# Modulation weights issued by GpSimd, the first token half routed inside the second half's output product, and second-map weights in another row order

## The reference, cut to what matters

```python
sh1, sc1, g1, sh2, sc2, g2 = split(silu(c) @ w_mod + b_mod, 6)   # w_mod 1024 x 6144
u = rmsnorm(x) * (1 + sc1) + sh1                                 # the context likewise
x_rnn, g_rnn, x_pool, m_rnn, m_pool = split(u @ w_in)
h = recurrent_states(x_rnn)          # 4 heads x 2 directions, gates by lru_wa, lru_wx
y_rnn = (h_f + h_b) * gelu(g_rnn);   y_pool = pool_mixer(x_pool)
merged = sigmoid(m_rnn) * (y_rnn @ w_rnn_proj) + sigmoid(m_pool) * (y_pool @ w_pool_proj)
x = x + g1 * rmsnorm(merged @ w_out)
v = rmsnorm(x) * (1 + sc2) + sh2
top_v, top_i = top_k(v @ w_r + b_r, 4)                           # of 32 experts
for e in range(32):
    z = v @ w1[e] + b1[e]            # 1024 x 2048
    act = clamped_swiglu(z)
    out += comb[:, e] * (act @ w2[e] + b2[e])                    # 1024 x 1024
x = x + g2 * rmsnorm(out)
```

## Time and profile before

| what | us |
|---|---|
| median of 3 runs (lowest, highest) | 1409.52 (1408.44, 1411.38) |
| the profiled execution | 1408.91 |
| its span | 1407.2 |
| TensorE busy | 1294.5 (92%) |
| VectorE busy | 348.0 (25%) |
| ScalarE busy | 215.9 (15%) |
| GpSimd busy | 19.3 (1%) |

### The profile page before, as it was taken

The page is one execution under the profiler, slowest core; times in us unless marked ns, Lnnn a source line. Parts: engine busy times, 40 slices in busy tenths (PEclk is TensorE's granted clock), DMA queues, the critical chain, the costliest instruction groups (busy, mean ns, idle before and its releaser), DMA issues.

```text
span 1407.2 us, 13120 instructions
## 1 busy us (share of the span) xinstructions
PE 1294.5 (92%) x5600; PEld 553.8 (39%) x5600; DVE 348.0 (25%) x605; ACT 215.9 (15%) x357; POOL 19.3 (1%) x58
## 2 busy tenths in 40 slices
PE   4999995699979999999999999999999999999995
PEld 2445684578643333333333333322333322333331
DVE  2457675332251112111211121111121111121112
ACT  3167530030011001000100010000010000010001
POOL 1000000000000000000000000000000000000000
PEclk9999997899968999999999999999999999999999
DMA  9322438999447999999999999999999999999994
GB/s 351 96 90 90 135 120 301 344 336 356 171 183 277 415 419 416 416 418 418 418 416 416 416 418 417 417 418 417 416 417 418 418 418 416 416 417 418 417 418 194
DMA packets 116905, 488.56 MB, mean 347 GB/s; under 512 B 9104, under 2 KB 43088, under 8 KB 79984
## 3 DMA queue, kind: packets, MB, share of 16 engines
q1 hardware_dynamic: 114768, 485.18, 86.2%
q0 software_dynamic: 544, 2.10, 0.4%
q10 hardware_dynamic: 1536, 0.46, 0.1%
HBM read 486.65 MB, written 1.05 MB: 347 GB/s over the span
## 4 chain that ended last, share of the span: by engine, by line
PE 43%; DMA 40%; DVE 6%; ACT 6%; SPq 4%; issue 1%; DVEq 0%; ACTq 0%
DMA arena<-in_exp_w 35%; PE bank L658 16%; PE bank L670 7%; PE bank L583 6%; SPq L361 3%; DMA arena<-in_w_in 3%; DMA arena<-in_w_mod 2%; PE bank L640 2%; PE bank L572 2%; PE bank L513 2%; PE bank L704 2%; PE bank L681 2%; ACT arena L822 1%; ACT arena L824 1%; ACT L816 1%
## 5 line engine op out<-in xcount | busy, mean ns | idle before, releaser
L658 PE MATMUL bank<-arena,temps 128*64 128x512 f32 x2112 | 472.8, 595 | 33.0 <-DMA arena<-in_exp_w 33.0
L658 PEld LDWEIGHTS bank<-arena,temps 128*64 128x64 f32 x2112 | 145.8, 137 | 354.4 <-issue 255.1
L670 PE MATMUL bank<-arena,temps 128*64 128x512 f32 x1056 | 233.9, 595 | 0.6 <-DVE temps L1239 0.6
L1232 DVE TENSOR_SCALAR temps<-bank 128x512 f32<-128x512 f32 x33 | 22.8, 692 | 750.1 <-PE bank L658 750.1
L583 PE MATMUL bank<-arena 128*128 128x256 f32 x512 | 119.2, 396 | 28.9 <-DMA arena<-in_w_in 28.9
L670 PEld LDWEIGHTS bank<-arena,temps 128*64 128x64 f32 x1056 | 72.6, 137 | 138.5 <-issue 132.5
L583 PEld LDWEIGHTS bank<-arena 128*128 128x128 f32 x512 | 101.9, 200 | 47.2 <-issue 32.3
L894 ACT ACTIVATE temps<-temps 128x512 f32<-128x512 f32 x33 | 20.8, 629 | 560.7 <-DVE temps L1232 560.7
L640 PE MATMUL bank<-vtokb,hot 128*64 128x512 f32 x264 | 67.4, 633 | 0.7 <-DVE hot L1174 0.7
L681 PE MATMUL bank<-temps,hot 64*128 64x512 f32 x264 | 65.6, 615 | 0.8 <-ACT temps L900 0.8
L704 PE MATMUL bank<-b1r,bsel 128*64 128x512 f32 x264 | 62.3, 592 | 0.6 <-issue 0.6
(11 more groups left out here) (229 smaller groups left out, 789.9 us busy)
## 6 DMA issues: line engine op xcount, KB each, us to landing
arena<-in_exp_w SPq DMA_DIRECT2D x396, 1024.0 KB, 22.0
arena<-in_w_mod SPq DMA_DIRECT2D x24, 1024.0 KB, 9.0
arena<-in_w_in SPq DMA_DIRECT2D x20, 1024.0 KB, 7.8
arena<-in_w_pool_proj SPq DMA_DIRECT2D x4, 1024.0 KB, 8.0
arena<-in_w_rnn_proj SPq DMA_DIRECT2D x4, 1024.0 KB, 6.6
arena<-in_w_out SPq DMA_DIRECT2D x4, 1024.0 KB, 10.2
arena<-in_lru_wa SPq DMA_DIRECT2D x8, 256.0 KB, 2.8
arena<-in_lru_wx SPq DMA_DIRECT2D x8, 256.0 KB, 3.1
```

Source lines behind the costliest of these rows:

```text
L658: last = mm(psum[4 + q][h * SLOTS:(h + 1) * SLOTS, :], xg[:, k // 4, k % 4, :], wslot[s][:, q, h * HALF:(h + 1) * HALF], start=False, stop ...
L670: last = mm(psum[6][h * SLOTS:(h + 1) * SLOTS, :], actT[:, k // 4, k % 4, :], wslot[s][:, kk, h * HALF:(h + 1) * HALF], start=(k == 0), st ...
L1232: v.tensor_scalar(glu, psum[4][:, :], LIMIT, None, ALU.min).then_inc(glu_ready, 1)
```

## The change

1. `gm` leaves `front_plan()` and the ring. GpSimd issues the 16 transfers after its constants, into four slots (`GM_SLOTS`: `ROWS_AT`, `M2`, `XC`, `XC + 1`), each once the product on that slot's former contents is done; from the eighth on (`GM_EARLY` = 7) also after the recurrence (`lru_done` = 8), since `XC` holds its input. VectorE does products 0 to 2 after the first three `conv`, 3 to 6 after steps 4 to 7, the rest after the pooling windows. ScalarE waits for `gm_done` = 7 before it writes `mp` into `M2`.
2. The product of the last quarter (t = 1, h = 1) is cut: k 0 and 1, then `vt` of half 0, k 2 to 5, `lg` of half 0, k 6 and 7, `rk` of half 0. ScalarE and VectorE take their parts in that order. `rk` becomes two jobs.
3. Ranks are kept from 1 and not from 0: `slotno` counts from 1 and the subtraction of 1 goes. `one_hot(0, 0)` moves ahead of the weights `comb`, and `neg_max` behind the mask.
4. Second-map weights: partition p holds rows 2p and 2p + 1 of each 256, and no longer rows p and 128 + p; the four turns of `actf` read every second column to match.

```diff
-RING_CHUNKS = 4 + 2 * HEADS + 4 + 12 + 16 + 1 + 8
-GM_AFTER = [0, 0, 1, 1, 2, 2, 2, 2, 2, 2, 1, 1]
+RING_CHUNKS = 4 + 2 * HEADS + 4 + 12 + 1 + 8
+GM_SLOTS = [ROWS_AT, M2, XC, XC + 1]
+GM_AT = [0, 1, 0, 1, 0, 1, 0, 2, 3, 0, 2, 3, 0, 2, 3, 0]
+GM_EARLY = 7
...
-        plan += [("vt", 2 * t, "A"), ("vt", 2 * t + 1, "V"), ("lg", t, "V")]
-    plan += [("rk", 0, "V"), ("ct", 0, "V")]
+        plan += [("vt", 2 * t, "A"), ("vt", 2 * t + 1, "V"), ("lg", t, "V"), ("rk", t, "V")]
+    plan += [("ct", 0, "V")]
...
-            return I["exp_w2"][0, ds(e, 1), r:r + 256, :].rearrange("a (k p) n -> p (a k) n", p=P)
+            return I["exp_w2"][0, ds(e, 1), r:r + 256, :].rearrange("a (p k) n -> p (a k) n", p=P)
...
-            link(g.iota(iotaI[:, :], pattern=[[64, 4], [0, 2], [1, 64]], base=0, channel_multiplier=0))
+            link(g.iota(iotaI[:, :], pattern=[[64, 4], [0, 2], [1, 64]], base=1, channel_multiplier=0))
...
+            pool.wait_ge(mod_used, KT)
+            for n in range(16):
+                k, h, q = n // 2, n % 2, GM_AT[n]
+                if n == GM_EARLY:
+                    pool.wait_ge(lru_done, 2 * HEADS)
+                if q in GM_AT[:n]:
+                    pool.wait_ge(gm_done, max(m for m in range(n) if GM_AT[m] == q) + 1)
+                pool.dma_start(slot(GM_SLOTS[q]), w_mod[k * P:(k + 1) * P, (h + 1) * CW:(h + 2) * CW]).then_inc(gm_landed[q], 16)
...
+                        wo(0, 0)
+                        wo(0, 1)
+                        wo(1, 0)
+                        wo(1, 1, 0, 2)
...
                     if n == 0:
+                        wo(1, 1, 2, 6)
                         pe.wait_ge(late_landed, 16 * 6)
...
+                elif kind == "rk" and n == 0:
+                    wo(1, 1, 6, KT)
+                    pe.wait_ge(mask_ready, 1)
+                    end_job(mm(b[:, 0:E], upper[:, :], mask[:, 0, :], start=True, stop=True))
                 elif kind == "rk":
...
+                    mm(b[:, 0:E], ones[:, :], mask[:, 0, :], start=True, stop=False)
+                    pe.wait_ge(mask_ready, 2)
+                    mm(b[:, 0:E], upper[:, :], mask[:, 1, :], start=False, stop=True)
+                    mm(b[:, E:2 * E], ones[:, :], mask[:, 0, :], start=True, stop=False)
+                    end_job(mm(b[:, E:2 * E], ones[:, :], mask[:, 1, :], start=False, stop=True))
...
-                    turned = nc.tensor.transpose(psum[7][:, j * P:(j + 1) * P], actf[:, j * P:(j + 1) * P], ident[:, :])
+                    turned = nc.tensor.transpose(psum[7][:, j * P:(j + 1) * P], actf[:, j // 2 * 256 + j % 2:j // 2 * 256 + 256:2], ident[:, :])
...
+                if kind == "mp":
+                    act.wait_ge(gm_done, GM_EARLY)
...
+            square_mix(0, 0)
+            square_mix(0, 1)
+            roots(0)
+            square_mix(1, 0)
+            take_turned(0)
+            square_mix(1, 1)
+            roots(1)
+            take_turned(1)
...
+            def mod_product(n):
+
+                k, h, q = n // 2, n % 2, GM_AT[n]
+                dve.wait_ge(gm_landed[q], 16 * GM_AT[:n + 1].count(q))
...
             for j in range(4):
                 conv(j)
+                if j < 3:
+                    mod_product(j)
...
                     conv(s + 4)
+                else:
+                    mod_product(s - 1)
...
+            for n in range(GM_EARLY, 16):
+                mod_product(n)
...
+            mix_half(0, 0)
+            tokens_of(0)
+            mix_half(1, 0)
+            route(0)
+            tokens_of(1)
+            take_rank(0)
+            route(1)
+            b = take_rank(1)
+            one_hot(0, 0)
+            v.tensor_copy(cnt, b[0:MORE, E:2 * E]).then_inc(read_dve, 1)
             dve.wait_ge(exps_ready, TT)
...
-            link(v.scalar_tensor_tensor(rank[:, :], b[:, 0:64], 1.0, mask.rearrange("p t e -> p (t e)"), ALU.add, ALU.mult))
-            link(v.tensor_scalar(rank[:, :], rank[:, :], -1.0, None, ALU.add))
```

More of the change, by code:

```diff
@@ L73, in front_plan @@
         plan += [("lru", s, None), ("xr", s + 4, "A") if s < 4 else ("xp", s - 4, "A")]
[L74 to L79, removed]
+    for kind in ("gg", "mr", "mp"):
+        plan += [(kind, c, "A") for c in range(4)]
     plan += [("pw", g, "A") for g in range(4)]
@@ L224, in build @@
         mod_landed = [sem(f"mod_landed{n}") for n in range(KT)]
+        gm_landed = [sem(f"gm_landed{q}") for q in range(4)]
         mod_used, mod_turned, gm_done, uT_act, uT_dve = (
@@ L503, in arrive, with wo @@
                 return chunk_of(kind, n)
[L505 to L513, removed]
-                                      wo_w[k // 2][:, k % 2, h * HALF:(h + 1) * HALF], start=(k == 0), stop=(k == KT - 1))
-                        last.then_inc(wo_done, 1)
+            def wo(t, h, k0=0, k1=KT):
+                for k in range(k0, k1):
+                    last = mm(psum[2 * t + h][:, :], mgT[:, k, t * P:(t + 1) * P],
+                              wo_w[k // 2][:, k % 2, h * HALF:(h + 1) * HALF], start=(k == 0), stop=(k == KT - 1))
+                if k1 == KT:
+                    last.then_inc(wo_done, 1)
             def mod_columns(k0, k1):
@@ L875, in _, with take_turned @@
                 a.activation(stat[:, 24 + t:25 + t], stat[:, 22 + t:23 + t], ACT.Sqrt).then_inc(root3, 1)
-            for t in range(TT):
+            def take_turned(t):
                 b = job_of("vt", 2 * t)
@@ L1117, in _, with one_hot, weighted, mix_half @@
                 v.tensor_tensor(m1[:, r], m1[:, r], m2[:, r], ALU.add).then_inc(merged_ready, 1)
-            for t in range(TT):
-                for h in range(2):
-                    dve.wait_ge(ssq2_ready, 2 * t + h + 1)
-                    r = slice(h * HALF, (h + 1) * HALF)
-                    ins = v.tensor_tensor(mG[:, t, r], psum[2 * t + h][:, :], row["g1"][:, r], ALU.mult)
+            def one_hot(e, r):
+                for t in range(TT):
+                    ins = v.tensor_scalar(sel[:, t, :], slotno[:, ds(r * 128, SLOTS)], rank[:, ds(e + t * E, 1)], None,
+                                          ALU.is_equal)
+                ins.then_inc(sel_ready, 1)
+            def weighted(e, r):
+                for t in range(TT):
+                    ins = v.tensor_scalar(selw[:, t, :], slotno[:, ds(r * 128, 128)], rank[:, ds(e + t * E, 1)],
+                                          comb[:, ds(e + t * E, 1)], ALU.is_equal, ALU.mult)
+                ins.then_inc(selw_ready, 1)
+            ib = ecol[:, 0:E].rearrange("p (k e) -> p k e", k=1).broadcast_to([P, TOPK, E])
+            def mix_half(t, h):
+                dve.wait_ge(ssq2_ready, 2 * t + h + 1)
+                r = slice(h * HALF, (h + 1) * HALF)
+                return v.tensor_tensor(mG[:, t, r], psum[2 * t + h][:, :], row["g1"][:, r], ALU.mult)
+            def tokens_of(t):
+                dve.wait_ge(ssq2_ready, 2 * t + 2)
                 link(v.tensor_tensor(stat[:, 12 + t:13 + t], small[:, 64 + 2 * t:65 + 2 * t], small[:, 65 + 2 * t:66 + 2 * t], ALU.add))
                 v.tensor_scalar(stat[:, 14 + t:15 + t], stat[:, 12 + t:13 + t], 1.0 / D, EPS, ALU.mult, ALU.add).then_inc(var2, 1)
+                link(mix_half(t, 1))
                 dve.wait_ge(root2, t + 1)
```

85 lines of the change are left out of this document (32 added, 53 removed).

## The result

| | us | range |
|---|---|---|
| before, median of 4 runs | 1408.98 | 1408.20 to 1411.38 |
| changed, median of 4 runs | 1369.64 | 1363.22 to 1373.25 |

The ratio is 0.9713 with a 95% interval of 0.9675 to 0.9751. The forecast was 1362 with 1354 to 1373 around it: the direction and the size are right, and the median is 7.6 us above the value. The profiled execution after took 1369.35 us (span 1367.3), so it stands at the median, and its span is 39.9 us shorter.

What follows compares the result with a forecast made beforehand. Expert-weight transfers bound the last stage, so its start and chunk pace count. From 1408.9 us: −36.8 + 0 − 11.2 + 0.3 + 0.3 = 1361.5, forecast as 1362 since the median is 0.6 above that execution; range 1354 to 1373.

Steps and rivals of the forecast that it cites:

- What bounds the kernel: Expert stage: DMA transfers of weights bound it, so its end follows the first freed slot plus 374 chunks at DMA pace.
- Part 1, modulation weights: Before the row sums: with the ring free, mr and mp run back to back, −36.8 us, bounds −27 and −38.
- 334 GB/s against the 417 that the engines reach: From 206 to 261 us: 18.4 MB over 55 us was claimed to fit the DMA engines, with less to spare.
- rival B: Before the row sums: modulation chunks are late, rs waits ten, expert stage starts 27 us sooner; 1372 us, chance 9%.
- The two rules weighed there: Modulation loads: another issuer saves only issue time; VectorE's two-port instructions starve GpSimd's DMA descriptors, a slip the 17 us cover.
- Part 2, routing: Output product to gather: routing half 0 inside half 1's product changes −0.4 to +1.3 us; value 0, bounds −4 and +2.
- mask + 4.75: Routing of half 1: the gather starts 4.75 us after the mask, against 3.7 before, because ct waits for comb.
- gather to first freed slot as unchanged: Between gather and first freed slot: both stretches, 7.57 and 1.94 us before, were forecast to stay the same.
- Part 3, piece size: Expert stage: 8 KB pieces save 0.09 us per second-map chunk, 124 chunks, −11.2 us, bounds −8 and −17.
- a term of 0.3 the other way: Start of the expert stage: the loss in the first item grows by about 0.3 us.
- my 0.3: Last item: the strided turns of actf, 0 to 0.66 us an item, paid once there; value +0.3 us.
- rivals A: Expert stage: A says packet size brings nothing to second-map chunks; 1373 us, chance 12%.

Runs made afterwards that it cites:

- rows late: The changed kernel with the seven row broadcast loads issued behind the pool_w chunk, at about 240 us and not 206: 1363.15 us, ratio 0.9682.
- modulation by SP: The changed kernel with the 16 modulation transfers issued by SP, not GpSimd, into the same four slots: 1363.11 us, ratio 0.9666.
- gather first: The changed kernel with TensorE doing gather(0) ahead of ct: 1368.41 us, ratio 0.9702.
- filler of 12 or 7: Matmuls without use where TensorE waits: twelve added to the changed kernel, 1365.61 us; seven added to the three edits, 1358.23 us.
- the three edits: The changed kernel with modulation transfers issued by SP, row broadcasts issued behind the pool_w chunk, and gather(0) ahead of ct: 1359.75 us, ratio 0.9648.

## Why the prediction was right, point by point

**What bounds the kernel.** Right. The span follows the first freed slot: with it at 388.4 to 408.6 us in the kernels that load the expert weights as the changed one does, the stretch to the last eighth chunk is 941 to 943.4 us each time, whatever was done before.

**Part 1, modulation weights.** The mechanism is right, the term mis-sized by 5.0 us (31.8 for 36.8), inside its bounds (27 to 38). The step that failed is "334 GB/s against the 417 that the engines reach". The bytes were as counted (326 GB/s over the 55 us), but most are asked for in the first 40, and chunks of `w_in` are cut in pieces of 1 KB. The engines were full at 386 GB/s from 206 to 245 us and less than half busy from 248. The prediction also had no term for two queues taking turns by the piece. The products themselves were in time (last one done at 245.6 for 251), so rival B, late modulation chunks, did not happen as I told it: what was late were the projections beside them.

**The two rules weighed there.** That issuing from another engine saves only issue time (the Trainium skill, "DMA: Bandwidth & Descriptors", "Issuing engines are not separate DMA queues") would have cost the whole term. The gain came from slots and places, as the run with SP shows, and to that extent the trace agrees: GpSimd's issuing brought nothing. Here it brought a loss of 6.5 us. That VectorE starves GpSimd's descriptors (the Trainium skill, "SBUF — State Buffer", "SBUF: two separate sides") was not seen: GpSimd's issues took 0.53 us each beside VectorE's products, and its six chunks landed in 8.3 us. Whether these products are the two-port instructions of that section no run shows.

**Part 2, routing.** Up to the gather right: 0.8 us less, for a forecast between 0.4 less and 1.3 more, with `ct` in front of the gather as the catch, shown by moving it (2.2 us). (The parts behind "mask + 4.75" add up to 4.6.) What I left out is the clock: I took gather to first freed slot as unchanged, and it cost 3.1 us. The clock's stretch at half speed lay over the bias and the start of the first map this time. The routing code alone is not the reason: the same code behind an earlier start (rows late, modulation by SP) lost nothing there. What set the moment of the clock's return stays open.

**Part 3, piece size.** The mechanism is right, and the total, 10.5 us for 10.9, is in part luck: the pieces bring 8.4 us, 0.07 us a chunk where I took 0.09, and the other 2.1 come from a better start of the stage, for which the sum has a term of 0.3 the other way. The price of the strided turns was 0.1 us at most for my 0.3.

**The sum.** 1361.5 became 1369.35: 5.0 in part 1, 3.1 in the clock, −0.8 in part 2, the rest below 0.5 each. The median lies inside the range because the two errors upward, 8 us together, are smaller than the 11 us of room above the value. That room was there for rivals A and B, and neither came true.

## What to carry to other kernels

Count bytes against the DMA engines in the stretch in which they are asked for, not over the whole stage, with the rate that their piece size allows; here the engines were full for 40 us inside a stage that had room on average. Before a load is given to another issuing engine, ask whose transfers it will share the engines with, and whose pieces are larger: here the same plan from one queue was 6.5 us faster. When a step is made early, follow the waiting engine's own order to the next instruction that needs it; an older wait may stand in front.

## What the runs showed of the hardware

- Two queues asking at once took turns by the piece and not by the byte: 294 packets each from 224 to 230 us, which gave the queue with 8 KB pieces 86.7% of the engines' time and the one with 1 KB pieces 14.2%. A chunk in SP's queue took up to 23.8 us to land then, for 11.2 (median) when all stood in one queue.
- Pieces of 8 KB move faster than pieces of 4 KB by 0.07 us a MiB (421 against 413 to 417 GB/s). The section "Specifications" of "DMA: Bandwidth & Descriptors" in the Trainium skill sets line rate from 512 bytes up; above that this case's whole stage differs by 1 to 2%, and a chunk whose pieces are all halved takes nearly 3% longer.
- A weight load of 128 columns at a stride of two float32 took 208 ns, and 143 without the stride.
- The clock can fall inside the last item: in three profiled executions (gather first, both with a filler of 12 or 7) the rest of the last item took 28.0 to 28.3 us and not 26.6. What decides when was not tried; the three edits without a filler, which also gather first, do not show it (26.6).
